# A retention head first with two first tiles together, sums of squares on VectorE, and the outputs of a layer's heads split by quarters of its last z tile

## What is computed

```python
mod = silu(c) @ w_ada + b_ada                 # 2048 x 6144, fp32
h = rmsnorm(x, g_norm) * (1 + scale) + shift
cols = h @ w_in                               # 16 heads: 4 hgrn2, 6 mlstm, 6 retention, and z
o = concat(heads(cols)) * silu(z)             # each head: chunked recurrence, norm, gain
y = x + gate * (o @ w_out)
```

## Time and profile before

| | |
|---|---|
| median of 3 runs | 2681.38 us (2676.97 to 2681.98) |
| profiled execution: its time | 2686.16 us |
| profiled execution: span | 2684.4 us |
| PE busy | 2476.5 us, 92% |
| DVE, ACT, POOL busy | 1194.7, 781.7, 942.4 us |
| mean granted TensorE clock | 0.975 |

### The profile page before, as it was taken

One profiled execution on the slowest core, in us unless ns is written; L12 is line 12 of the kernel. 1 busy time (PEld: TensorE's weight loads), 2 busy tenths in 40 slices (PEclk: granted clock), 3 DMA queues, 4 the chain that ended last, 5 costly groups with the idle time before them and its releaser, 6 DMA issues.

```text
span 2684.4 us, 48465 instructions
## 1 busy us (share of the span) xinstructions
PE 2476.5 (92%) x20538; PEld 2236.0 (83%) x20538; DVE 1194.7 (45%) x2280; ACT 781.7 (29%) x1223; POOL 942.4 (35%) x676
## 2 busy tenths in 40 slices
PE   3776999799999999989999799979999999998998
PEld 2115999689999999987777599969999999998998
DVE  2004555457776433341000555536766743344444
ACT  1004322233343333341111422223343333333111
POOL 0002434134443344354222233323443444445542
PEclk9998999999999999999999899989999999999999
DMA  4995333233333443328887333323333333432542
GB/s 167 323 317 165 80 96 84 62 81 103 83 97 101 110 113 102 101 65 267 287 283 250 102 91 95 82 59 90 87 97 97 103 105 105 112 90 66 142 115 87
DMA packets 473266, 339.70 MB, mean 127 GB/s; under 512 B 17749, under 2 KB 416561, under 8 KB 471729
## 3 DMA queue, kind: packets, MB, share of 16 engines
q1 hardware_dynamic: 473050, 336.61, 43.2%
HBM read 304.72 MB, written 32.04 MB: 125 GB/s over the span
## 4 chain that ended last, share of the span: by engine, by line
PE 76%; DVE 8%; DMA 7%; ACT 3%; DVEq 2%; POOL 2%; issue 1%; SPq 1%; ACTq 0%
PE pj L535 59%; DMA raw<-in_w_ada 4%; PE mx L541 2%; PE mx L745 2%; DMA raw<-in_w_out 2%; POOL wlo L506 1%; PE pj L616 1%; ACT whi L896 1%; PE mx L570 1%; PE mx L601 1%; PE mx L544 1%; DVE t L1132 1%; PE mx L759 1%; PE mx L655 1%; DVEq L1225 1%
## 5 line engine op out<-in xcount | busy, mean ns | idle before, releaser
L506 POOL TENSOR_TENSOR wlo<-raw,whi 128x512 fp32r<-128x512 f32 x640 | 899.9, 1438 | 1704.8 <-ACT whi L896 1704.8
L535 PE MATMUL pj<-hh,whi 128*128 128x260 f32 x5120 | 1068.8, 290 | 62.0 <-POOL wlo L506 33.6
L535 PE MATMUL pj<-hh,wlo 128*128 128x260 f32 x5120 | 1038.1, 285 | 0.0
L535 PE MATMUL pj<-hl,whi 128*128 128x260 f32 x5120 | 1036.9, 284 | 0.0
L535 PEld LDWEIGHTS pj<-hh,whi 128*128 128x128 f32 x5120 | 794.8, 190 | 139.9 <-issue 101.6
L535 PEld LDWEIGHTS pj<-hl,whi 128*128 128x128 f32 x5120 | 796.9, 190 | 0.0
L535 PEld LDWEIGHTS pj<-hh,wlo 128*128 128x128 f32 x5120 | 796.4, 190 | 0.0
L896 ACT ACTIVATE whi<-raw 128x2048 fp32r<-128x2048 f32 x160 | 306.3, 1916 | 316.9 <-DMA raw<-in_w_out 173.0
L896 ACT ACTIVATE xv<-pj 128x260 f32<-128x260 f32 x192 | 66.3, 384 | 433.7 <-PE pj L535 433.4
L1132 DVE SCALAR_TENSOR_TENSOR o<-pj,mod,t 128x260 f32<-128x260 f32 x64 | 28.0, 480 | 343.3 <-PE pj L535 343.1
L616 PE MATMUL pj<-raw,sct 128*32 128x512 f32 x384 | 100.3, 645 | 45.8 <-DMA raw<-in_w_ada 45.7
(11 more groups left out here) (242 smaller groups left out, 2243.4 us busy)
## 6 DMA issues: line engine op xcount, KB each, us to landing
raw<-in_w_in SPq DMA_DIRECT2D x256, 512.0 KB, 5.2
raw<-in_w_ada SPq DMA_DIRECT2D x96, 512.0 KB, 5.3
raw<-in_w_out SPq DMA_DIRECT2D x64, 512.0 KB, 6.1
lev<-in_w_ada SPq DMA_DIRECT2D x58, 512.0 KB, 4.8
xv<-in_w_ada SPq DMA_DIRECT2D x38, 512.0 KB, 5.1
out<-ss SPq DMA_DIRECT2D x32, 512.0 KB
y_kept<-o SPq DMA_DIRECT2D x2, 4160.0 KB, 12.8
t<-y_kept SPq DMA_DIRECT2D x32, 260.0 KB, 4.8
```

The lines of the kernel that those rows point to most:

```text
L506: last = e.tensor_tensor(wlo[:, par, cs], w[:, cs], whi[:, par, cs].bitcast(F32), ALU.subtract)
L535: last = e.matmul(pj[:, 2 * par + b, 0:HALF], w[:, par, kb * P:(kb + 1) * P], x[:, kb, b * HALF:(b + 1) * HALF], start=(kb == 0 and m == 0 ...
```

## The change

It has four parts.

1. **Sums of squares on DVE.** `square(n)` squares chunk n and adds it to `zw` on DVE. In layer 0 this runs during the `w_ada` product, in layer 1 during the output product of layer 0 (16 times, behind each `out_added`). PE's `norm` becomes two matmuls, in layer 0 placed after group 5 of `w_ada`. ACT's 16 squares go. DVE starts on h straight behind `ag`; layer 1's small `lb` steps move behind the h chunks. ACT's `high` of the first two tiles moves ahead of them: in layer 1 to the very start of the layer, ahead of the copies of `prm` and `bia`.
2. **A retention head first, with its first two tiles together.** `KINDS` becomes 1 retention, 4 hgrn2, 6 mlstm, 5 retention. The loads, counters and slots follow; the rope table is loaded one more time per layer. PE waits for `lo_done` of both first tiles, and then takes each chunk of h for both tiles, 12 matmuls, before it waits for the next.
3. **The finished outputs are split by quarters of the last z tile.** `z_quarter` is raised after eighths 1, 3 and 5; ACT then makes `hh` of chunks 0 to 11 ahead of the take of z, DVE makes `hl` of chunks 0 to 3 (ahead of its wait for the states), POOL makes `hl` of 4 to 11, then `wlo` of output tile 1, then the rest.
4. **Output tiles 0 and 1** run three quarters each one after the other; `back` follows the first quarter of tile 1.

```diff
-KINDS = ["hg"] * H_HG + ["ml"] * H_ML + ["rt"] * H_RT
+KINDS = ["rt"] + ["hg"] * H_HG + ["ml"] * H_ML + ["rt"] * (H_RT - 1)
...
                 fetch(0)
+                if l == 0:
+                    e.wait_ge(lm_taken, 1)
+                else:
+                    e.wait_ge(ada_used, 2 * ADA_GROUPS * ADA_PIECES)
+                e.dma_start(rope_t, rope_d).then_inc(rope_in, 16)
...
-                for kb in range(KB):
+                for kb in range(LOW_FIRST, 12):
+                    low_o(l, kb)
+                low(l * TILES + 4 * NH + 1, 1)
+                for kb in range(12, KB):
                     low_o(l, kb)
...
-                for kb in range(KB):
-                    e.wait_ge(sq_ready, n * KB + kb + 1)
-                    for b in range(2):
-                        last = e.matmul(mx[:, b, 0:HALF], ones, (t1, t2)[kb % 2][:, b * HALF:(b + 1) * HALF],
-                                        start=(kb == 0), stop=(kb == KB - 1))
-                    last.then_inc(sq_used, 1)
+                e.wait_ge(sq_acc, n + 1)
+                for b in range(2):
+                    last = e.matmul(mx[:, (2, 3)[b] if n == 0 else (0, 3)[b], 0:HALF], ones,
+                                    zw[:, b * HALF:(b + 1) * HALF], start=True, stop=True)
+                last.then_inc(sq_sum, 1)
...
                 tile_wait(t0, 0, l * NH)
-                for part in range(4):
-                    last = quarter(0, part, h_ready, l)
-                last.then_inc(tile_done, 1)
+                tile_wait(t0 + 1, 1, l * NH)
+                for kb in range(KB):
+                    e.wait_ge(h_ready, l * KB + kb + 1)
+                    last = [quarter(par, kb, parts=KB) for par in range(2)]
+                last[0].then_inc(tile_done, 1)
+                last[1].then_inc(tile_done, 1)
...
-                    for j in range(1, 4):
+                    for j in range(1 if h else 2, 4):
                         tile(t, j, g, own[j - 1])
...
-                for part in range(3):
-                    for n in range(2):
+                for n in range(2):
+                    for part in range(3):
                         out_part(n, part)
-                        if (n, part) == (0, 1):
+                        if (n, part) == (1, 0):
                             late[5][0]()
...
             for l in range(DEPTH):
+                if l:
+                    for j in range(2):
+                        high(l * TILES + j, l * TILES // 2 + 1, j)
                 e.wait_ge(prm_tr, l + 1)
...
                         e.wait_ge(head_done, g + 1)
+                        if h + 1 == NH:
+                            for kb in range(12):
+                                e.wait_ge(z_quarter, 3 * l + kb // 4 + 1)
+                                high_o(l, kb)
                         take(3, z, 0)
...
+            def square(n):
+
+                tt(zw[:] if n == 0 else z[:], o[:, n, :], o[:, n, :], M)
+                e.drain()
+                if n:
+                    tt(zw[:], zw[:], z[:], A_)
+                    e.drain()
...
+                        if h + 1 == NH:
+                            for kb in range(LOW_FIRST):
+                                e.wait_ge(o_hi, l * KB + kb + 1)
+                                tt(hl[:, kb, :], o[:, kb, :], hh[:, kb, :].bitcast(F32), S_).then_inc(o_lo_first, 1)
                         e.wait_ge(ps["u"], g + 1)
```

More of the change, by code:

```diff
@@ L53 @@
 LOW_CUT = 4
+LOW_FIRST = 4
 TILES = 4 * NH + KB
@@ L87, in stores_before @@
     per_layer = 3 + sum(STORES[k] for k in KINDS)
-    return l * per_layer + 1 + sum(STORES[k] for k in KINDS[:h]) + (2 if h > H_HG else 0)
+    return l * per_layer + 1 + sum(STORES[k] for k in KINDS[:h]) + (2 if h > FIRST_ML else 0)
 def constants():
@@ L273, in fin_freed, with scorec @@
             e.wait_ge(fin_dve if i % 2 else fin_act, i // 2 + 1)
[L275 to L280, removed]
+        def scorec(l, h, x):
+            per = [LEVELS + 1 if k == "hg" else 1 for k in KINDS]
+            return l * sum(per) + sum(per[:h]) + x
         def fold(m):
@@ L306, in head_of, with same_parity, o_ready @@
             kind = KINDS[h]
-            i = h - BASE[kind]
+            i = KINDS[:h].count(kind)
             return kind, i, i + l * COUNT[kind], l * NH + h, l * TILES + 4 * h
+        def same_parity(g):
+            l, h = divmod(g, NH)
+            return sum(KINDS[x % NH] == KINDS[h] and x % 2 == g % 2 for x in range(g + 1))
+        def o_ready(e, l, kb):
+            if kb < LOW_FIRST:
+                e.wait_ge(o_lo_first, l * LOW_FIRST + kb + 1)
+            else:
+                e.wait_ge(o_lo, l * (KB - LOW_FIRST) + kb - LOW_FIRST + 1)
         def ht(g, j):
@@ L637, in tile @@
                             last.then_inc(tile_done, 1)
+                        elif part % 2 and j == 3 and g % NH == NH - 1:
+                            last.then_inc(z_quarter, 1)
                         for hook in hooks.get(part, ()):
@@ L945, in _ @@
                     ada_take(n, (t1, t2), pj, 0)
-                e.wait_ge(mod_ready, l + 1)
+                    if n == 5:
+                        norm(0)
+                if l:
+                    norm(l)
+                else:
+                    for j in range(2):
+                        high(j, 1, j, False)
+                for kb in range(KB):
+                    e.wait_ge(hn_ready, l * KB + kb + 1)
+                    act(hh[:, kb, 0:T], (t1, t2)[kb % 2][:, 0:T], ACT.Identity, bias=mod[:, kb, 0:1]).then_inc(h_hi, 1)
                 if l:
@@ L954, in _ @@
                     act(lbv[:], lbc[:, 0:2, :], ACT.Exp).then_inc(lb_exp, 1)
[L955 to L960, removed]
                 def gates():
@@ L1167, in _, with norm @@
             e.wait_ge(const_in, 32)
[L1168 to L1171 removed]
+            ts(lmask[:], levf[:, 0:LEVELS * 128], 0.5, None, ALU.is_gt).then_inc(lm_taken, 1)
+            def square(n):
[4 more added lines that the diff above has]
+                    e.drain()
+            def norm(n):
+                e.wait_ge(sq_sum, n + 1)
                 for b in range(2):
[L1173 removed]
+                    ts(t3[:, b * HALF:(b + 1) * HALF], mx[:, (2, 3)[b] if n == 0 else (0, 3)[b], 0:HALF], 1.0 / D, EPS, M, A_)
                 e.drain().then_inc(ms_ready, 1)
[L1176 removed]
+            e.wait_ge(sct_taken, 2)
+            for kb in range(KB):
+                e.wait_ge(xt_taken, kb + 1)
+                square(kb)
+            e.sem_inc(sq_acc, 1)
+            norm(0)
             for l in range(DEPTH):
@@ L1184, in _ @@
                 stt(ag[:], mod[:, KB:2 * KB, :], 1.0, bc(prm[:, R_NORM:R_NORM + KB], 2, 9), A_, M).then_inc(mod_ready, 1)
+                e.memset(x0[:, 0:PAD], 0.0)
+                e.memset(x1[:, 0:PAD], 0.0)
+                if l:
+                    norm(l)
+                e.wait_ge(rs_made, l + 1)
+                hs = t4[:, 0:KB * NS].rearrange("p (k s) -> p k s", s=NS)
+                tt(hs, o[:, :, T:TOK], bc(t3[:, T:TOK], 1, KB), M)
+                e.drain()
+                tt(hs, hs, ag[:, :, 1:9], M)
+                e.drain()
+                tt(hs, hs, mod[:, 0:KB, 1:9], A_)
+                e.drain()
+                e.tensor_copy(hh[:, :, T:TOK], hs)
+                e.drain()
+                tt(hl[:, :, T:TOK], hs, hh[:, :, T:TOK].bitcast(F32), S_).then_inc(hs_ready, 1)
+                for kb in range(KB + 1):
+                    if kb < KB:
+                        stt((t1, t2)[kb % 2][:, 0:T], o[:, kb, 0:T], ag[:, kb, 0:1], t3[:, 0:T], M, M).then_inc(hn_ready, 1)
+                    if kb:
+                        e.wait_ge(h_hi, l * KB + kb)
+                        stt(hl[:, kb - 1, 0:T], (t1, t2)[(kb - 1) % 2][:, 0:T], mod[:, kb - 1, 0:1],
+                            hh[:, kb - 1, 0:T].bitcast(F32), A_, S_).then_inc(h_ready, 1)
+                    e.drain()
                 lb0, lb1 = prm[:, R_LB:R_LB + H_HG], prm[:, R_LB + H_HG:R_LB + 2 * H_HG]
@@ L1283, in _ @@
                         ss, hc, nr = ss2[:, g % 2], hc2[:, g % 2], nr2[:, g % 2]
-                        gain = prm[:, R_GN + h:R_GN + h + 1]
+                        gain = prm[:, R_GN + BASE[kind] + i:R_GN + BASE[kind] + i + 1]
                         def log_sigmoid(dst, src, name):
```

106 lines of the change are left out of this document (40 added, 66 removed).

## The result

The changed kernel takes 2644.02 us (median of 4 runs, 2638.07 to 2646.83) against 2681.68 before (4 runs beside it); the ratio is 0.9856, 95% interval 0.9842 to 0.9871. The forecast was 2644.2. The profiled execution took 2643.58 us, span 2641.8. That is 42.6 us less than the profiled execution before, 5 more than the medians say.

What follows compares the result with a forecast made beforehand. PE, busy 92% of the span, bounds the kernel; only its waits or low-clock stretches can give time. 2.1 + 21.5 + 5.8 + 7.8 = 37.2 us takes the median from 2681.4 to 2644.2, range 2627 to 2662.

Steps and rivals of the forecast that it cites:

- Layer 0's start: Start of layer 0: first hh only 5.6 us earlier, held by late weight loads; gains 2.1 us.
- the restart: PE coming back slow after a pause: 2.4 us lost over 72 matmuls, counted as 2.3.
- The new wait: Behind the pair, each layer: PE stands still 10.0 us while tile 2's weights are made, plus 2.3 of slow matmuls.
- Rival B: Behind the pair: no wait, PE finds tile 2's weights ready; 12.3 us more per layer, 2619.6; chance 0.05.
- Layer 1's start: Start of layer 1, from PE's last output matmul to tile 2: gains 21.5 us, bounds 17 and 26.
- End of the heads, layer 0: PE's idle before the output product goes, 9.3 us, cut by the w_ada load to a gain of 5.8.
- End, layer 1: End of layer 1's heads, decided by output tile 2's load and weights: gains 7.8 us, bounds 5 and 9.
- Rival A: Ends of heads: four hl delay states 1.3 us per layer, layer 0's 5.8 lost to loads; 2652.6; chance 0.20.
- lock-out of whole instructions: DVE's four hl beside POOL: if all take turns, states come 2 to 3 us late per layer, gain about 32.
- C: Start of layer 1: early norm does nothing, h starts 10 us later than forecast; 2654; chance 0.08.
- D: Pair and two tiles after the stop run at the low clock: 32.4 us per layer, 2709; chance 0.03.
- E: Head order makes a hook wait about 9 us per layer and ends give nothing: 2676 or so; chance 0.04.

Runs made afterwards that it cites:

- e6: Changed kernel with the y_kept and conv_s stores issued behind the first weight loads instead of ahead of them: 2639.45 us, ratio 0.9836.
- e4: Kernel before with part 1 alone (squares on DVE, early high; hgrn2 first, one first tile, old ends): 2647.06 us, ratio 0.9874.
- e5: Changed kernel, but in each layer's first head ACT makes whi of tile 2 before taking tile 0's six copies: 2642.43 us.
- e1: Changed kernel without the pair: first tile takes the chunks of h alone, retention head still in front: 2643.44 us, ratio 0.9856.
- e11: Same kernel as e1 (one first tile, no pair), measured again in more rounds beside the changed kernel: 2634.8 us.
- e2: Changed kernel with the old end of the heads put back (parts 3 and 4 undone): 2653.26 us, ratio 0.9893.
- e3: Kernel before with the new end of the heads alone (parts 3 and 4): 2670.89 us, ratio 0.9961.

## Why the prediction was right, point by point

- **Layer 0's start.** First `hh` at 229.1 forecast, 228.71 measured; the pair from 237.3 to 262.7, measured 237.23 to 262.28; tile 2 at 272.7 (before the restart), measured 272.40. Gain 2.1, measured 1.8 on the mean of three (983.0, 983.9, 984.0 against 985.4 and 985.6). e6 shows that the loads behind the store were the cause, e4 that without the pair the same start gives 9.5.
- **The new wait.** 10.0 forecast, 10.12 in both layers, with some luck. The chain from ACT's first take to the end of `low` took 10.7 us, as POOL's `low` took 6.37 beside DVE's rope operations, not 5.52. But ACT took tile 0 already 0.7 us before the pair ended. e5 shows that take, high and low stand in a row (2.8 us less). Rival B fell. What the prediction did not ask is what one first tile alone would do. The last chunk of h was ready at 256.4 in layer 0, where the pair ended at 262.28, and at 1492.55 in layer 1, where it ended at 1495.2. One tile needs 0.7 us behind the last chunk, and 11.55 for the other tile. So the pair brought 6.4 and 9.6 us, and paid 10.1 of stop and about 2 of restart in each layer (an estimate from these rows: 5.7 and 2.5 us lost; against the mean of the three profiles with the pair e1 and e11 measured 6.5 and 5.2 in layer 0, 2.5 and 2.8 in layer 1).
- **Layer 1's start.** 21.5 forecast, 20.5 measured in the stretch. The mis-sized term is the way from PE's last output matmul to the first chunk: 12.3 forecast, 15.0 measured. DVE's timeline in the changed kernel shows the last square and its addition both stretched beside POOL, where I had stretched one, and so was one of the five samples' operations:

```profile
1457.73 1.64 DVE L1155 TENSOR_TENSOR z<-o 128x520 f32<-128x520 f32 x1
1459.44 1.61 DVE L1155 TENSOR_TENSOR zw<-zw,z 128x520 f32<-128x520 f32 x1
...
1466.13 1.20 DVE L1155 TENSOR_TENSOR t<-t,ag 128x128 f32<-128x128 f32 x1
```

  PE's norm took 2.1 us, for which the sum held only the 1.0 of `mod` and `ag`, which run beside it. The stretch misses by less than these 2.7 us, because the pair took 24.5 us where I had 25.4, and because 0.7 us of the delay fall before the transpose of `prm` from which the stretch is counted.
- **End of the heads, layer 0.** 5.8 forecast, 6.9 measured over all profiles. `head_done` reached SP 13.6 us behind the hook's end instead of 19.6, 6.0 sooner, forecast 5.8, and PE waits for the load as forecast. What I carried through the output product at 5.8 is as uncertain as its spread of 9 us.
- **End, layer 1.** 7.8 forecast, 6.4 measured. POOL's `wlo` of output tile 2 took 5.85 us beside the squares, not 5.1, and the load landed 4.8, not 5.8, sooner. For both ends together the prediction had 13.6 and the stretches say 13.3, but the medians of e2 and e3 say 9.2 and 11.8; this difference stays open.
- **Rival A** was right in place and wrong in size: the last hook did wait for the states, 0.34 us in layer 0 and 0.35 in layer 1, where the rival had 1.3. The four `hl` took 5.66 us. Three were stretched beside POOL, to 1.59, 1.83 and 1.78 us, where I had priced two at 1.63; the second took 0.69, as it fell into POOL's pause from 1182.88 to 1183.94. The Trainium skill's lock-out of whole instructions ("SBUF — State Buffer", section "Who interferes with whom") had given about 8 us for the four by the prediction's sum, and states 2 to 3 us late. The trace agrees that the two engines hold each other up, but not with that sum. The rival's other half, layer 0's share lost in waits for loads, did not come.
- **C, D and E** fell: layer 1's h started 2.7 us late, not 10; the clock was up again inside the pair (0.93 in 240 to 250); and the retention head in front costs no hook a wait of 9 us (e1 and e11 against e4: 977.1, 978.4 against 975.9; 964.8, 964.5 against 965.0). For D the prediction had misread its ground. It had the clock at 0.50 through the whole stretch of single chunks, from a window that ends at 250. The next windows of the kernel before show it back up while PE still waited for chunks:

```profile
250.00:260.00 10.00, 7.25 (x44) 5.82 (x42) 9.35 (x15) 4.50 (x8) 0.00 (x0) 0.95 0.39 94
260.00:270.00 10.00, 8.44 (x65) 7.80 (x64) 4.18 (x6) 6.35 (x9) 1.90 (x2) 1.00 0.01 2
```

The total agreed to 0.2 us, which is luck within a spread of some 9 us between runs. The errors of the four terms (-0.3, -1.0, +1.1, -1.4) cancel in part, and the stretches sum to 35.6, where the medians say 37.7.

Still open: why the `w_ada` stage ends anywhere from 205.4 to 218.2 us with the same products in it. Nothing was tried on it.

## What to carry to other kernels

When two products that used to follow each other are made to end together, ask what was prepared under the second. Here the pair brought 6 to 10 us per layer and paid 10 us of stop and about 2 of restart, and running the two tiles one after the other, or staggered, was faster. A step taken off the critical path pays only down to what is late next, here loads queued behind a store that nobody yet waited for; issuing the store behind them brought their first use 9.6 us forward. And where one stage of a kernel varies by more than an edit is worth, compare the stretch that the edit is in, mark to mark, before believing an equal total.

## What the runs showed of the hardware

The `w_ada` stage, bound by its loads, differs between executions by 12.8 us. In windows from 50 us to its end, the slow one (e1) and the fast one (e6):

```profile
50.00:218.20 168.20, 119.78 (x486) 29.15 (x485) 14.77 (x22) 8.81 (x16) 0.00 (x0) 0.89 0.87 297
50.00:205.40 155.40, 109.39 (x486) 26.01 (x486) 14.67 (x23) 8.81 (x16) 0.00 (x0) 1.00 0.91 312
```

The slow one had a granted clock of 0.89 and 297 GB/s, the fast one 1.00 and 312. The same view of all 14 profiles goes the same way: at 0.95 and above the stage ended between 205.4 and 210.8, at 0.93 between 211.6 and 213.4, at 0.91 and below between 214.7 and 218.2. Whether the clock falls because PE waits for loads, or the loads are asked for later because PE is slow, these views can't tell.
